# Recurrent mixer: two passes of half visits become one stage of 34 visits

## The reference

```python
def step(S, inp):
    qc, kc, vc, lf = inp
    b = jnp.cumsum(lf, axis=1)
    diff = b[:, :, None] - b[:, None, :]
    decay = jnp.exp(jnp.where(causal, diff, -jnp.inf))
    a = jnp.einsum('bthk,bshk,btshk->bhts', qc, kc, decay)
    o = (jnp.einsum('bhts,bshv->bthv', a, vc)
         + jnp.einsum('bthk,bhkv->bthv', qc * jnp.exp(b), S))
    b_last = b[:, -1]
    S_new = (jnp.exp(b_last)[..., None] * S
             + jnp.einsum('bshk,bshv->bhkv', kc * jnp.exp(b_last[:, None] - b), vc))
    return S_new, o
...
o_f, s_f = _hgrn_chunk_scan(q, k_f, v, lf_f, s0_f)
o_b, s_b = _hgrn_chunk_scan(q[:, ::-1], k_b[:, ::-1], v[:, ::-1], lf_b[:, ::-1], s0_b)
o_hg = rms_norm(o_f + o_b[:, ::-1], hg_norm_l.reshape(HG_HEADS, HG_DV))
o_hg = (o_hg * jax.nn.silu(heads(hg_g.astype(jnp.float32), HG_HEADS))).reshape(B, N, HG_WIDTH)
```

## Time and profile before

| | |
|---|---|
| median of three runs | 3680.49 us (3672.06 to 3681.95) |
| the profiled execution | 3675.72 us |
| its span, first to last instruction | 3674.0 us |
| TensorE busy | 3192.9 us, 87% |
| VectorE busy | 2008.1 us, 55% |
| ScalarE, GpSimd busy | 1200.0 us, 503.2 us |
| mean granted TensorE clock | 0.873 |
| recurrence, both passes | 1230.6 to 1793.3 us |

### The profile page before, as it was taken

One profiled execution on the slowest core, in us unless ns is written; L12 is line 12 of the kernel. 1 busy time (PEld: TensorE's weight loads), 2 busy tenths in 40 slices (PEclk: granted clock), 3 DMA queues, 4 the chain that ended last, 5 costly groups with the idle time before them and its releaser, 6 DMA issues. The chain is left out here.

```text
span 3674.0 us, 51533 instructions
## 1 busy us (share of the span) xinstructions
PE 3192.9 (87%) x19551; PEld 2749.0 (75%) x19551; DVE 2008.1 (55%) x4328; ACT 1200.0 (33%) x2056; POOL 503.2 (14%) x732
## 2 busy tenths in 40 slices
PE   8579999977999888899689933999999999999990
PEld 1258888855666687788668833999999999999990
DVE  3541113215776588788434457666666566666644
ACT  0431124312444322222133301444444444444422
POOL 3312101012110000022101100021111112211102
PEclk9679999987999766555789955999999999999995
DMA  7533222126563210110132324466555556665528
GB/s 269 160 116 114 96 75 96 68 73 140 122 122 74 68 44 22 61 44 30 43 121 110 109 110 139 146 189 198 184 184 172 181 177 188 198 191 178 168 81 315
DMA packets 283930, 474.98 MB, mean 129 GB/s; under 512 B 41295, under 2 KB 179206, under 8 KB 280166
## 3 DMA queue, kind: packets, MB, share of 16 engines
q1 hardware_dynamic: 256984, 380.08, 32.7%
q0 software_dynamic: 24192, 83.80, 8.2%
q10 hardware_dynamic: 2592, 8.98, 0.6%
HBM read 373.50 MB, written 99.49 MB: 129 GB/s over the span
## 5 line engine op out<-in xcount | busy, mean ns | idle before, releaser
L2296 DVE TENSOR_TENSOR ex_wlow<-ex_w,ex_whigh 128x2048 fp32r<-128x2048 f32 x192 | 440.2, 2293 | 159.1 <-ACT ex_whigh L2236 158.9
L2236 ACT ACTIVATE ex_whigh<-ex_w 128x2048 fp32r<-128x2048 f32 x192 | 366.7, 1911 | 253.0 <-DMA ex_w<-in_w_up 141.6
L2124 PE MATMUL ex_Y<-ex_hs_high,ex_whigh 128*128 128x272 f32 x1024 | 302.9, 296 | 17.2 <-DVE ex_hs_low L2312 17.2
L2124 PE MATMUL ex_G<-ex_xs_high,ex_whigh 128*128 128x272 f32 x1024 | 301.2, 294 | 2.3 <-DVE ex_xs_low L2280 2.3
L2126 PE MATMUL ex_G<-ex_xs_high,ex_wlow 128*128 128x272 f32 x1024 | 297.4, 290 | 0.0
L2126 PE MATMUL ex_Y<-ex_hs_high,ex_wlow 128*128 128x272 f32 x1024 | 297.1, 290 | 0.0
L2124 PE MATMUL ex_U<-ex_xs_high,ex_whigh 128*128 128x272 f32 x1024 | 296.7, 290 | 0.0
L2126 PE MATMUL ex_U<-ex_xs_high,ex_wlow 128*128 128x272 f32 x1024 | 296.4, 289 | 0.0
L2125 PE MATMUL ex_G<-ex_xs_low,ex_whigh 128*128 128x272 f32 x1024 | 295.7, 289 | 0.0
L2125 PE MATMUL ex_Y<-ex_hs_low,ex_whigh 128*128 128x272 f32 x1024 | 295.4, 288 | 0.0
L2125 PE MATMUL ex_U<-ex_xs_low,ex_whigh 128*128 128x272 f32 x1024 | 294.8, 288 | 0.0
(11 more groups left out here) (351 smaller groups left out, 7842.3 us busy)
## 6 DMA issues: line engine op xcount, KB each, us to landing
ex_w<-in_w_gate SPq DMA_DIRECT2D x64, 1024.0 KB
ex_w<-in_w_up SPq DMA_DIRECT2D x64, 1024.0 KB
ex_w<-in_w_down SPq DMA_DIRECT2D x64, 1024.0 KB
wada<-in_ada_w SPq DMA_DIRECT2D x12, 2048.0 KB, 8.2
hg_rows<-hg_pool_rows SPq DMA_DIRECT2D x68, 256.0 KB, 3.1
hg_pool_rows<-hp_res POOLq DMA_DIRECT2D x34, 384.0 KB, 2.8
hp_w<-in_w_in SPq DMA_DIRECT2D x48, 256.0 KB
at_q_parts<-queries_keys SPq DMA_DIRECT2D x16, 544.0 KB, 7.3
```

The source lines that it names most:

```text
L2124: nc.tensor.matmul(out, wh, xh, start=start, stop=False)
L2236: nc.scalar.activation(h, v, ACT.Copy).then_inc(s_high, 1)
L2296: nc.vector.tensor_tensor(l, v, h, ALU.subtract).then_inc(s_low, 1)
```

## The change

`hg_pass`, called twice, becomes `hg_mixer`, called once. It visits the tiles 34 times, first forwards and then backwards, without a barrier, a new head and a new load of masks between. A visit handles all four heads:

- One operation of VectorE or GpSimd covers both head pairs. Queries and keys lie so in `QK` that readers and sources of a level come from one access pattern (`kq`), so one multiply makes a whole level.
- The sum over five levels goes. The centred product is masked into the score matrix, the first level is copied over its quarter, and three predicated copies put the other levels in their places.
- A level's matmul makes only the columns of its readers, at all four levels; the matmuls alternate between the heads j = 0 and j = 1, whose scores lie in different halves of a PSUM area.
- The state is kept as 128 x 64, without zero blocks. The outputs use it one head at a time (`past`), in half-height matmuls, and the increment is made from keys that are padded with zeros (`KH`).
- The centred product and the keys' product move from VectorE to GpSimd (`centred`, `keys_after`).
- `o_fwd` lies in a part of `mixT` that only the pooling mixer uses later. The masks are loaded once for both directions, without VectorE's cast.

The core of the diff (the loop of ScalarE is that of the half visits, in the new order; `hg_masks` is no longer called here):

```diff
-def hg_pass(nc, g, a, out, hgp, masks_d, rev, o_fwd):
+def hg_mixer(nc, g, a, out, hgp, masks_d):
...
+        KH = m.sb("hg_KH", [P, 3, 2, 2, P])
+        AS = m.sb("hg_AS", [P, 2, 4, P])
+        S = m.sb("hg_S", [P, 2, 2, 2, HD])
+        pA = [m.ps(f"hg_pA{i}", (P, 4, 256)) for i in range(2)]
...
+                for d in range(2):
+                    sp.dma_start(sums[:, d].bitcast(F32), masks_d[:, d * HG_MASKS:d * HG_MASKS + 7, :]).then_inc(s_masks, 16)
+                    sp.dma_start(keep[:, d], masks_d[:, d * HG_MASKS + 7:(d + 1) * HG_MASKS, :]).then_inc(s_masks, 16)
...
+                def centred(v):
+                    pool.wait_ge(s_exp, 2 * v + 2)
+                    pool.wait_ge(s_qk, v + 1)
...
+                    nc.gpsimd.tensor_tensor(Z8[:, v % RZ], EX[:, v % RE, 5:7], QK[:, v % 2], ALU.mult).then_inc(s_z8, 1)
...
+                    nc.gpsimd.tensor_tensor(own, heads(kk[:, v % R, :]), heads(EY[:, v % 2, :]), ALU.mult).then_inc(s_kh, 1)
...
+                for v in range(-1, V + 1):
+                    if v + 1 < V:
+                        centred(v + 1)
+                        keys_after(v + 1)
+                    if v - 1 >= T:
+                        normalise(v - 1 - T)
...
+                    pe.wait_ge(s_z8, v + 1)
+                    pe.wait_ge(s_z, v + 1)
+                    if v >= 1:
+                        pe.wait_ge(s_as, v)
+                    for hp in range(2):
+                        for j in range(2):
+                            r = rows_of(j)
+                            nc.tensor.matmul(pA[0][:, 2 * j + hp, 0:P], z8[r, 1 - rd, hp, :], z8[r, rd, hp, :], start=True, stop=True)
+                    for l in range(4):
+                        bank, c = AREA[1 + l]
+                        for hp in range(2):
+                            for j in range(2):
+                                r = rows_of(j)
+                                last = nc.tensor.matmul(pA[bank][:, 2 * j + hp, c], z[r, l, hp, :], half(z[r, l, hp, :], l, rd), start=True, stop=True)
...
+                    past(0).then_inc(s_p0, 1)
+                    pe.wait_ge(s_as, v + 1)
+                    for h in range(4):
+                        nc.tensor.matmul(pOU[:, h * HD:(h + 1) * HD], AS[:, v % 2, 2 * (h % 2) + h // 2, :], vv[:, x, h * HD:(h + 1) * HD], start=False,
+                                         stop=(h % 2 == 0), skip_group_check=True)
+                    pe.wait_ge(s_p0, v + 1)
+                    past(1).then_inc(s_o, 1)
...
+                for v in range(V + 1):
+                    if v + 1 < V:
+                        exponents(v + 1, 0)
+                    if v + 2 < V:
+                        to_features(v + 2)
+                    if v >= 1:
+                        outputs(v - 1)
+                    if v + 1 < V:
+                        exponents(v + 1, 1)
+                    if v < V:
+                        pairs(v)
+                    if v - 3 >= T:
+                        to_mix(v - 3 - T)
...
-                    for l in range(4):
-                        half = lambda ap: ap.rearrange("p (b w h) -> p w b h", w=2, h=P >> (l + 1))
-                        for w, x in ((reader, q), (source, k)):
-                            nc.vector.tensor_tensor(half(Z[:, b, l, :])[:, w], half(EX[:, n % 3, 1 + l, :])[:, w], half(x)[:, w], ALU.mult)
...
+                        kq = bass.AP(QK[:, v % 2].tensor, QK[:, v % 2].offset, [[1024, P], [2 * h, P // h], [256 + h, 2], [1, h]])
+                        last = nc.vector.tensor_tensor(parts(Z[:, b, l]), parts(e[:, 1 + l]), kq, ALU.mult)
...
-                    nc.vector.tensor_reduce(AS[:, n % 2], AM[:, :, :, :].rearrange("p j l t -> p j t l"), AX.X, ALU.add).then_inc(s_as, 1)
...
+                    nc.vector.tensor_tensor(into, pA[0][:, :, 0:P], keep[:, d, 4, :].unsqueeze(1).to_broadcast([P, 4, P]), ALU.mult).then_inc(s_m8, 1)
...
+                    nc.vector.tensor_copy(into[source, :, 64 * rd:64 * rd + 64], pA[0][source, :, P:P + 64]).then_inc(s_m8, 1)
...
+                        nc.vector.copy_predicated(into.rearrange("p x (b w h) -> p x w b h", w=2, h=h)[:, :, rd], kept,
+                                                         pA[1][:, :, AREA[1 + l][1]].rearrange("p x (b h) -> p x b h", h=h)).then_inc(s_as if l == 3 else s_m8, 1)
```

More of the change, by code:

```diff
@@ new lines, in hg_mixer @@
+        T = TILES
+        V = 2 * T
+        R = 6
+        RE, RZ, RO = 3, 2, 4
+        SPAN = (CTX_TILE, *range(LAT_TILES)), (CTX_TILE, *range(LAT_TILES)[::-1])
+        sums = m.sb("hg_sums", [P, 2, 7, P], F32R)
+        keep = m.sb("hg_keep", [P, 2, 5, P])
+        rows = m.sb("hg_rows", [P, R, 5, HG_W])
+        lf, kk, vv, gg, qq = (rows[:, :, x, :] for x in range(5))
+        lfH, lfL = m.sb("hg_lf_high", [P, 2, HG_W], F32R), m.sb("hg_lf_low", [P, 2, HG_W], F32R)
+        QK = m.sb("hg_QK", [P, 2, 2, 2, P])
@@ L803, in hg_pass, with tile, state, half @@
+        def tile(v):
+            return SPAN[rev(v)][v % T]
+        def state(v):
+            return S[:, rev(v), CTX if v % T == 0 else LAT]
+        def half(ap, l, w):
+            return ap.rearrange("p (b w h) -> p w b h", w=2, h=P >> (l + 1))[:, w]
         with nc.Block() as block:
@@ new lines, in _ @@
+                for v in range(V):
+                    if v >= R:
+                        sp.wait_ge(s_o, v - R + 1)
+                        if rev(v - R):
+                            sp.wait_ge(s_n2, v - R - T + 1)
+                    r = v % R
+                    for x, n, slot in ((0, 2, 3 if rev(v) else 1), (2, 2, 5), (4, 1, 0)):
+                        sp.dma_start(rows[:, r, x:x + n, :], hgp[tile(v), :, slot:slot + n, :]).then_inc(s_in[r], 16)
+                    if v == 0:
+                        for d in range(2):
+                            for h in range(4):
+                                j, hp = h % 2, h // 2
+                                sp.dma_start(S[64 * j:64 * j + 64, d, LAT, hp, :], a["state_hgrn"][0, 0, d, h]).then_inc(s_s0, 16)
+                    if v % T == R:
+                        sp.wait_ge(s_st, v - R + 1)
@@ L1003, in _ @@
-                if rev:
-                    mixes(T - 2)
-                    mixes(T - 1)
+                exps(0, 0)
+                features(1)
+                exps(0, 1)
+                for v in range(V + 1):
+                    if v + 1 < V:
+                        exps(v + 1, 0)
+                    if v + 2 < V:
+                        features(v + 2)
+                        high_part(v + 2)
+                    if 1 <= v <= T:
+                        forward_out(v - 1)
+                    if v + 1 < V:
+                        exps(v + 1, 1)
+                    if v - 3 >= T:
+                        mixes(v - 3 - T)
@@ new lines, in update @@
+                def update(v):
+                    dve.wait_ge(s_o, v + 1)
+                    last_col = 0 if rev(v) else P - 1
+                    for hp in range(2):
+                        last = nc.vector.scalar_tensor_tensor(out=state(v)[:, hp, :], in0=state(v)[:, hp, :],
+                                                              scalar=EX[:, v % RE, 0, hp, last_col:last_col + 1],
+                                                              in1=pOU[:, 256 + hp * HD:256 + (hp + 1) * HD],
@@ L1079, in _ @@
                 weigh(0)
[L1080 to L1090 removed]
+                for v in range(V + 1):
+                    if v >= 1:
+                        update(v - 1)
+                        if rev(v - 1):
+                            finish(v - 1)
+                    if v + 2 < V:
+                        low_part(v + 2)
+                    if v < V:
+                        mask(v)
+                    if v >= 1 and rev(v - 1):
+                        squares(v - 1)
+                    if v + 1 < V:
+                        weigh(v + 1)
 def pool_mixer(nc, g, a, hgp, masks_d):
```

387 lines of the change are left out of this document (155 added, 232 removed).

## The result

The changed kernel takes 3431.89 us (median of 4 runs, 3416.65 to 3445.51) against 3676.72 beside it: a ratio of 0.9333, 95% interval 0.929 to 0.9375. The forecast was 3434. The profiled execution is the fastest of these runs, 3416.65 us with a span of 3414.6. Four later runs took 3436.47 to 3443.96.

A forecast was written before the change was run, and what follows sets the result against it. VectorE's loop and low-clock TensorE were taken to bound the mixer. Head 14.9, visits 3 x 15.3 + 31 x 8.1 and tail 9.2 make 321.1 us against 562.7, giving 3434; range 3389 to 3480, or 3385 to 3545 with two rivals.

The forecast's parts named there:

- Two owners: Mixer before: VectorE's loop and TensorE filled at the low clock both own the period of 15.6 us a visit.
- The rival of a bound GpSimd: Reverse visits: GpSimd's multiplies stretch 2.9 times, 9.6 us a visit, 25 us more, total 3460; chance 0.13.
- What the prediction said against it: GpSimd's multiplies: VectorE's masking reads PSUM, and the multiplies fall beside it.
- the lower bound of 2.1: TensorE's pairs in a high-clock visit: 2.1 us if the two halves run as two full streams.
- outputs with seams: TensorE's outputs at the high clock: 2.73 us for 24 passes, plus 0.4 for gaps around half-height passes.
- the rest: TensorE's exponents and transposes in a visit: 2.20 us at the high clock, half of the low clock's 4.40.
- the slower rival: TensorE's pairs: alternating halves do not overlap and the clock stays low, 18.0 us a visit, 3749 us; chance 0.04.
- the compact state costs TensorE's path: TensorE's outputs: 24 passes instead of 16, costing 1.7 us a visit at the low clock.
- Three low visits: Mixer: three of 34 visits at the low clock, 15.3 us each, the rest high at 8.1.
- where TensorE is kept fed it stays up: TensorE's clock in the mixer: it falls after idling and stays high when fed, as in 2400 to 2600 us.
- the 5 allowed: Mixer's head, up to the first pairs: left at 14.9 us, within 5.
- tail: Mixer's end, from the last outputs to the next stage: 9.2 us.

The follow-up runs named there:

- 3: The kernel before, with only the pairs of the two 64-row halves made to alternate: 3664.99 us, ratio to before 0.9962.
- 10: The kernel before, with the first exponent product of each head pair computed twice: 3671.43 us, ratio to before 0.9987.
- 2: The changed kernel with the sum over five levels put back on VectorE in place of the predicated copies: 3609.57 us, ratio to before 0.9803.
- 1: The changed kernel with the pairs of each 64-row half in runs instead of alternating: 3496.36 us once, 3561.33 to 3564.30 three times.
- 5: The changed kernel with GpSimd's two multiplies a visit back on VectorE: 3436.98 us, ratio to before 0.934.
- 7: The changed kernel with the halves in runs, not alternating, and the first exponent product of each head pair computed twice: 3516.98 us.
- 6: The changed kernel with two of four levels of pairs computed for all 128 columns instead of 64: 3421.29 us, ratio to before 0.9293.
- 4: The changed kernel with the compact state undone, block-diagonal 128x128 a head pair again: 3371.04 us, ratio to before 0.916.
- experiment 11: The changed kernel itself, run again unaltered: 3439.39 us, ratio to before 0.9357.
- 9: The changed kernel with the sum over levels back on VectorE and the first exponent product computed twice: 3634.19 us, against 3609.57 with the sum alone.
- 8: The changed kernel with the block-diagonal state and SyncE's load queue in another order: 3369.47 us, ratio to before 0.9151.

## Why the prediction was right

**Bound before.** Two owners: shown. The overlap alone brings 15 us (3), and a clock of 0.75 for 0.61, with more work, some 6 (10). Taken out of the change, the relief of VectorE costs 178 (2) and the overlap some 60 in the fastest run (1). So each needs the other to show its worth.

**VectorE.** The predicated copy costs 0.443 us, forecast 0.42; the 512-element product 0.692, forecast 0.68. The visit's work is 4.8 and 5.5 us (80.48 and 91.61 us over 16.7 and 16.5 visits), forecast 5.4 and 6.5. The durations were right and their sum too large: four products that last 0.43 each stand 1.42 us in the timeline, so neighbours overlap, and busy time counts that once.

**GpSimd.** 1.27 and 0.74 us against 1.23 and 0.61, and nobody waits for its multiplies. The rival of a bound GpSimd fell: 80.37 us of 133.40, without the stretching it rested on. What the prediction said against it holds, since the multiply falls beside VectorE's masking (1302.26 and 1302.19 us in a forward visit). In the head, where it met VectorE's products (from 1249.39), the four took 3.04 us instead of 1.42:

```profile
1249.63 3.04 DVE L1086 TENSOR_TENSOR hg_Z<-hg_EX,hg_QK 128x256 f32<-128x256 f32 x4
...
1305.17 1.42 DVE L1086 TENSOR_TENSOR hg_Z<-hg_EX,hg_QK 128x256 f32<-128x256 f32 x4
```

The need for the move fell as well (5).

**TensorE.** The visit was forecast 8.1 us and is 7.89 forward, 8.07 in reverse. Its terms: pairs 2.38 for 2.8, nearer to the lower bound of 2.1 than to the value taken; outputs with seams 3.14 for 3.13; the rest 2.37 for 2.20. That the halves overlap when they alternate is shown by experiment 1 (3.54 us apart, and 3.53 in 7), and so the slower rival falls. That columns are worth nothing here is shown by 6. That the compact state costs TensorE's path was forecast; it costs 1.43 us a visit at 1.00, 0.91 for passes and the rest for seams (4).

**The clock.** Three low visits (45.9 us) were forecast. Of the visits some 13 us are low in the profiled run (2 x 0.03 x 132.3 + 2 x 0.02 x 133.4) and some 46 in experiment 11. A low visit was put at 15.3 us and takes 14.24. So the term's size fits one of the two profiled runs, but its reason was half right. Where TensorE waits for VectorE, the stage's mean clock is 0.61 to 0.75 in every run here; added work lifts it from 0.61 to 0.75 in 10 and hardly in 9 (0.69 to 0.70). The step "where TensorE is kept fed it stays up" is the one that failed: in experiment 11 the clock falls from 1.00 to 0.50 in a TensorE that has been busy without a pause for over 100 us. What makes it fall there, and how often it does, these runs don't show.

**The sum.** Head 22.1 us for 14.9, 7.2 over and outside the 5 allowed. The masks that lead the queue are the smaller part: TensorE's first transposes start 9.2 us into the stage (1240.78) for 7.8 before, and another order of the queue gains 3 us (8). From there to the first pairs it is 12.9 us for 7.1 before, counted from this row of before to 1245.50:

```profile
1238.37 1.12 PE L862 MATMUL hg_pT<-ident,hg_rows 128*128 128x128 f32 x4 [11.46 <-DMA hg_rows<-hg_pool_rows]
```

The changed code puts the exponents of four head pairs ahead of the first pairs, where before had those of two; the prediction left that out. Visits 269.9 (1253.68 to the last outputs at 1523.54) for 297.0; tail 12.7 for 9.2. Together 304.7 for 321.1, in the fastest run; 318.1 in experiment 11. That the median comes within 3 us of the forecast is in part luck: visits 27 us shorter and head and tail 11 longer than summed, and the profiled execution, the one the sum was made for, is 17 us under the forecast.

## What to carry to other kernels

When two engines own a period, try each relief alone before believing in either: here the one brought 15 us and the other, taken away, cost 178, and together they bring 245. Where matmuls use half the rows, alternate the two halves matmul by matmul, and pay for a compact layout only after counting the passes that it adds on the engine that will be the bound; here it cost 44 to 61 us. A cut in columns, and work moved off an engine with slack, bought nothing here.

## What the runs showed of the hardware

The granted clock can fall from 1.00 to 0.50 while TensorE is busy in every microsecond (16.00 of 16.00 us at 0.50 in experiment 11, after 8.00 of 8.00 at 1.00). Which property of the work in it brings that about, these runs don't settle. A change between half-height and full-height passes costs some 0.14 us at 1.00, without any wait in the code. Passes of 64 columns took 0.057 us each with the halves alternating and, with half of them widened to 128, 0.059. A predicated copy of 256 elements from PSUM cost 443 ns, about a plain product's 416 (L1031 in the earlier trace rows).
